# Odd attention of a two-block model: two copies change engine, and score buffers and maxima go round in longer rings

## What is computed

```python
def odd_mixer(x, w_in, w_out, ...):
    q_c, kv_c, gate_c, cq, ckv, k_rope = split_cols(x @ w_in, ODD_SPLITS)
    ...
    o_cmp, slc_score = nsa_compressed(q, kv[:, :, 0, 0], kv[:, :, 0, 1], cmp_pe, cmp_w1, cmp_w2, tbl_c)
    o_slc = nsa_selected(q, kv[:, :, 1, 0], kv[:, :, 1, 1], slc_score, tbl_c)
    o_win, _ = banded_attention(q, kv[:, :, 2, 0], kv[:, :, 2, 1], WIN_SIZE - 1, tbl_c, 1)
    o_c = gates[:, :, 0] * o_cmp + gates[:, :, 1] * o_slc + gates[:, :, 2] * o_win
    ...
    o_d = mla_attention(qd[..., :D_NOPE], rope(qd[..., D_NOPE:], pos), k_nope, rope(k_rope, pos), v)
    y = jnp.concatenate([o_c.reshape(B, S, -1), o_d.reshape(B, S, -1)], axis=-1)
    return y @ w_out
```

## Time and profile before

| | |
|---|---|
| median of three runs | 2121.37 us (2120.21 to 2123.31) |
| the profiled execution | 2128.46 us, its span 2126.7 us |
| TensorE busy | 2008.8 us, 94% of the span |
| VectorE busy | 1089.1 us, 51% |
| ScalarE busy | 959.7 us, 45% |

### The profile page before, as it was taken

One profiled execution on the slowest core, in us unless ns is written; L12 is line 12 of the kernel. 1 busy time (PEld: TensorE's weight loads), 2 busy tenths in 40 slices (PEclk: granted clock), 3 DMA queues, 4 the chain that ended last, 5 costly groups with the idle time before them and its releaser, 6 DMA issues.

```text
span 2126.7 us, 25345 instructions
## 1 busy us (share of the span) xinstructions
PE 2008.8 (94%) x9889; PEld 1494.4 (70%) x9889; DVE 1089.1 (51%) x2023; ACT 959.7 (45%) x1758; POOL 12.7 (1%) x28
## 2 busy tenths in 40 slices
PE   8999889999889999889999999999889999999997
PEld 3876446677456888566788888787655678888885
DVE  5623864632774322656655543442465576555333
ACT  4734664644674333574422222344676544322223
POOL 1000000000000000000000000000000000000000
PEclk8999889999989999999999999999999999999999
DMA  8431432223202533003233333324400123333331
GB/s 280 128 81 50 159 99 79 60 71 90 80 20 80 149 89 92 8 1 114 70 99 99 93 97 93 104 77 100 142 2 1 41 70 99 99 93 96 99 92 47
DMA packets 301268, 183.14 MB, mean 86 GB/s; under 512 B 17550, under 2 KB 292108, under 8 KB 299948
## 3 DMA queue, kind: packets, MB, share of 16 engines
q1 hardware_dynamic: 295437, 166.05, 26.7%
q10 hardware_dynamic: 4704, 13.31, 1.7%
q0 software_dynamic: 1008, 2.15, 0.3%
HBM read 179.22 MB, written 2.27 MB: 85 GB/s over the span
## 4 chain that ended last, share of the span: by engine, by line
PE 82%; DVE 8%; ACT 6%; issue 2%; DMA 1%; another core or an unknown queue 0%; ACTq 0%; DVEq 0%
PE PS L902 22%; PE PS L904 22%; PE PS L903 21%; PE PS L1048 3%; PE PS L1076 2%; PE PS L1061 2%; DVE SE L2152 1%; DVE WLO L2078 1%; PE PS L1202 1%; PE PS L1120 1%; PE PS L1225 1%; PE PS L1129 1%; PE PS L1014 1%; DVE X L2045 1%; ACT WHI L1514 1%
## 5 line engine op out<-in xcount | busy, mean ns | idle before, releaser
L903 PE MATMUL PS<-LO,WHI 128*128 128x512 f32 x1690 | 659.8, 390 | 0.0
L902 PE MATMUL PS<-HI,WHI 128*128 128x512 f32 x1578 | 626.6, 397 | 25.2 <-DVE LO L2051 10.3
L904 PE MATMUL PS<-HI,WLO 128*128 128x512 f32 x1578 | 616.7, 391 | 0.0
L2078 DVE TENSOR_TENSOR WLO<-RING,WHI 128x1024 fp32r<-128x1024 f32 (+3 forms) x271 | 314.3, 1160 | 530.9 <-ACT WHI L1514 529.9
L1514 ACT ACTIVATE WHI<-RING 128x1024 fp32r<-128x1024 f32 (+3 forms) x271 | 272.6, 1007 | 468.6 <-PE PS L904 446.7
L902 PEld LDWEIGHTS PS<-HI,WHI 128*128 128x128 f32 x1578 | 297.6, 189 | 108.5 <-issue 27.0
L903 PEld LDWEIGHTS PS<-LO,WHI 128*128 128x128 f32 x1690 | 318.5, 188 | 65.3 <-issue 1.7
L904 PEld LDWEIGHTS PS<-HI,WLO 128*128 128x128 f32 x1578 | 297.3, 188 | 62.9
L902 PE MATMUL PS<-HIDDEN,WHI 128*128 128x512 f32 x352 | 137.1, 390 | 0.6 <-PE PS L904 0.6
L904 PE MATMUL PS<-HIDDEN,WLO 128*128 128x512 f32 x352 | 137.0, 389 | 0.0
L903 PE MATMUL PS<-HIDDEN,WHI 128*128 128x512 f32 x352 | 136.9, 389 | 0.0
(11 more groups left out here) (341 smaller groups left out, 2343.1 us busy)
## 6 DMA issues: line engine op xcount, KB each, us to landing
RING<-in_ffn_w_up SPq DMA_DIRECT2D x88, 512.0 KB, 3.7
RING<-in_w_in SPq DMA_DIRECT2D x48, 512.0 KB, 3.8
RING<-in_w_mod SPq DMA_DIRECT2D x32, 512.0 KB, 4.3
RING<-in_ffn_w_down SPq DMA_DIRECT2D x32, 512.0 KB, 4.0
RING<-in_ev_w_in SPq DMA_DIRECT2D x30, 512.0 KB, 3.8
RING<-in_w_out SPq DMA_DIRECT2D x16, 512.0 KB, 4.4
RING<-in_od_w_in SPq DMA_DIRECT2D x15, 512.0 KB, 3.9
RING<-in_ffn_w_down SPq DMA_DIRECT2D x16, 384.0 KB, 3.4
```

The source lines that it names most:

```text
L902: mm(bank, WHI[i2][:, i, :], hi, start=(k == 0), stop=False)
L903: mm(bank, WHI[i2][:, i, :], lo, start=False, stop=False)
L904: return mm(bank, WLO[i2][:, i, :], hi, start=False, stop=last)
L2078: tt(WLO[i2][:, 0:nk, :], raw, WHI[i2][:, 0:nk, :], ALU.subtract).then_inc(me.signals(w_split), 1)
```

## The change

In the odd attention, VectorE takes two kinds of copies over from ScalarE: that of the small turn of each gated unit (`small_collected`), and that of the mixed values of each unit (`mixed`). The copies of a turned bank are now counted on two semaphores, `at_turn_free` for ScalarE's and `at_small_free` for VectorE's; `bank_left` says which of them a turn has to wait for. There is a third set of maxima, for both attentions. The odd attention's units go round in seven score buffers, by `SE_ODD`, where buffer 3 comes twice in eight; the three new ones lie in tiles of Z that are free in this stage, and in RS, which is made longer by 128 columns. ScalarE's `high`, which used to follow its own `mixed`, waits on `at_mixed`.

```diff
-        RS = sb("RS", [T])[:, :]
+        RS_WIDE = sb("RS", [640])
+        RS = RS_WIDE[:, 0:T]
...
-        UNIT_MAX = [TINY[:, c:c + 8] for c in (56, 152)]
+        UNIT_MAX = [TINY[:, c:c + 8] for c in (56, 152, 104)]
...
+        SE += [spare("SE4", ends["Z"] + 31 * TILE, [3 * T]), spare("SE5", ends["Z"] + 10 * TILE, [5 * T]), RS_WIDE]
+        SE_ODD = (0, 1, 2, 3, 4, 5, 6, 3)
...
+        def collected_through(at):
+            return SMALL_TURN[:at].count(False), SMALL_TURN[:at].count(True)
+
+        def bank_left(at):
+            n = max((n + 1 for n in range(at) if TURN_BANK[n] == TURN_BANK[at]), default=0)
+            if n:
+                by_act, by_dve = collected_through(n)
+                return (at_small_free, by_dve) if SMALL_TURN[n - 1] else (at_turn_free, by_act)
...
+                u["se"] = u["n"] % 4 if u["n"] < len(UNITS["even_mix"]) else SE_ODD[u["n"] % 8]
+                u["before"] = filled.get(u["se"])
+                filled[u["se"]] = u
...
                 def values(u):
-                    pe.wait_ge(at_turn_free, u["turned"])
+                    by_act, by_dve = collected_through(u["turned"])
+                    pe.wait_ge(at_turn_free, by_act)
+                    if u["gates"]:
+                        pe.wait_ge(at_small_free, by_dve)
...
                 def high(k):
-                    act.wait_ge(*me.last)
+                    if even:
+                        act.wait_ge(*me.last)
+                    else:
+                        act.wait_ge(at_mixed, len(UNITS["even_mix"]) + 4 * (k + 1))
                     inputs([H[:, k, :]], even and k < 4, k, HI_MIXED)
...
                 for i in range(n + 5):
-                    if 0 <= i - 5 < n:
+                    if even and 0 <= i - 5 < n:
                         mixed(units[i - 5])
...
-                        if x < len(turns):
+                        if x < len(turns) and not (units[i - 3]["gates"] and x == 0):
                             collect(units[i - 3], x)
...
                 def scaled(u):
-                    if u["n"] >= 4:
-                        dve.wait_ge(at_turned, every[u["n"] - 4]["turned"])
-                    buf, nmax = SE[u["n"] % 4][:, 0:2 * u["width"]].rearrange("p (a t) -> p a t", a=2), UNIT_MAX[u["n"] % 2]
-                    if u["n"] >= 2:
-                        dve.wait_ge(at_exp, every[u["n"] - 2]["exps"])
+                    if u["before"]:
+                        dve.wait_ge(at_turned, u["before"]["turned"])
+                    buf, nmax = SE[u["se"]][:, 0:2 * u["width"]].rearrange("p (a t) -> p a t", a=2), UNIT_MAX[u["n"] % 3]
+                    if u["n"] >= 3:
+                        dve.wait_ge(at_exp, every[u["n"] - 3]["exps"])
...
+                def small_collected(u):
+                    dve.wait_ge(at_turned, u["turn"] + 1)
+                    if u["ring"] >= 10:
+                        dve.wait_ge(at_values, OWNER[u["ring"] - 10]["done"])
+                    nc.vector.tensor_copy(ET_SLOTS[u["place"] % 10][0:31, 0:2, :],
+                                          PS[0:31, TURN_BANK[u["turn"]], 0:2 * B].rearrange("p (x q) -> p x q", x=2)) \
+                        .then_inc(at_small_free, 1)
+
+                def mixed(u):
+                    dve.wait_ge(at_values, u["done"])
+                    nc.vector.tensor_copy(u["dst"], PS[:, 7, 0:B]).then_inc(me.signals(at_mixed), 1)
...
-                for i in range(n + 2):
+                for i in range(n + 2 if even else n + 5):
                     if i < n:
                         scaled(units[i])
-                    if i >= 2:
+                    if not even and i >= 5:
+                        mixed(units[i - 5])
+                    if 0 <= i - 3 < n and units[i - 3]["gates"]:
+                        small_collected(units[i - 3])
+                    if 0 <= i - 2 < n:
                         normalise(units[i - 2])
```

More of the change, by code:

```diff
@@ L318, in build @@
         acc_ready, acc_free_act, acc_free_dve = sem("acc_ready"), sem("acc_free_act"), sem("acc_free_dve")
+        at_small_free = sem("at_small_free")
         at_scores, at_scaled, at_exp, at_probs, at_turned, at_turn_free, at_values, at_mixed = (
@@ L661, in build @@
         UNITS = {"even_mix": even_units(), "odd_mix": odd_units()}
-        OWNER, TURN_BANK = [], []
-        def turns_collected(at):
-            return max((n + 1 for n in range(at) if TURN_BANK[n] == TURN_BANK[at]), default=0)
+        OWNER, TURN_BANK, SMALL_TURN = [], [], []
+        def collected_through(at):
[5 more added lines that the diff above has]
+                return (at_small_free, by_dve) if SMALL_TURN[n - 1] else (at_turn_free, by_act)
         def count_units():
             n_unit = n_score = n_scaled = n_exp = n_prob = n_value = 0
-            mains, sides = [], []
+            mains, sides, filled = [], [], {}
             for u in UNITS["even_mix"] + UNITS["odd_mix"]:
                 u["n"], n_unit = n_unit, n_unit + 1
+                u["se"] = u["n"] % 4 if u["n"] < len(UNITS["even_mix"]) else SE_ODD[u["n"] % 8]
+                u["before"] = filled.get(u["se"])
+                filled[u["se"]] = u
                 for g in u["groups"]:
@@ L689, in count_units @@
                 OWNER.extend([u] * len(u["turns"]))
+                SMALL_TURN.extend(bool(u["gates"]) and i == 0 for i in range(len(u["turns"])))
                 TURN_BANK.extend(5 + (u["turn"] + i) % 2 for i in range(len(u["turns"])))
@@ L1055, in turn @@
                     at = u["turn"] + i
-                    if turns_collected(at):
-                        pe.wait_ge(at_turn_free, turns_collected(at))
-                    buf = SE[u["n"] % 4]
+                    if bank_left(at):
+                        pe.wait_ge(*bank_left(at))
+                    buf = SE[u["se"]]
                     for x, (a, c, w) in enumerate(u["turns"][i]):
@@ L1639, in exp @@
                     c += a * u["width"]
-                    x = SE[u["n"] % 4][:, c:c + w]
-                    fn(x, x, ACT.Exp, bias=UNIT_MAX[u["n"] % 2][:, at:at + 1], scale=-1.0,
+                    x = SE[u["se"]][:, c:c + w]
+                    fn(x, x, ACT.Exp, bias=UNIT_MAX[u["n"] % 3][:, at:at + 1], scale=-1.0,
                         accum_out=UNIT_DEN[u["n"] % 3][:, at:at + 1]).then_inc(at_exp, 1)
@@ L1951, in _ @@
                     elif s in ("even_out", "odd_out"):
+                        if s == "odd_out":
+                            act.wait_ge(at_mixed, sum(len(units) for units in UNITS.values()))
                         inputs(inputs_of(s)[-1:], False, len(inputs_of(s)) - 1, HI_MIXED)
@@ L2155, in normalise @@
                 def normalise(u):
-                    buf, den, rden = SE[u["n"] % 4], UNIT_DEN[u["n"] % 3], UNIT_RDEN[u["n"] % 2]
+                    buf, den, rden = SE[u["se"]], UNIT_DEN[u["n"] % 3], UNIT_RDEN[u["n"] % 2]
                     dve.wait_ge(at_exp, u["exps"])
@@ L2182, in normalise @@
                         ts(buf[:, c:c + w], buf[:, c:c + w], rden[:, at:at + 1], None, ALU.mult).then_inc(me.signals(at_probs), 1)
+                def small_collected(u):
[7 more added lines that the diff above has]
+                    dve.wait_ge(at_values, u["done"])
+                    nc.vector.tensor_copy(u["dst"], PS[:, 7, 0:B]).then_inc(at_mixed, 1)
                 def head_scaled():
```

## The result

| | before | after |
|---|---|---|
| median | 2120.45 us (five runs) | 2103.34 us (five runs, 2099.73 to 2106.03) |
| ratio, 95% interval | | 0.9909 [0.9894, 0.9923], so 16 to 22 us less |
| the profiled execution, its span | 2128.5, 2126.7 | 2106.0, 2104.2 |
| VectorE, ScalarE busy | 1089.1, 959.7 | 1102.0, 949.5 |

Faster, as forecast, but by more. The forecast was 2108.6 us, in a range of 2103 to 2117, on a base of 2121.4. By the ratio that base becomes 2102.1 us, 19.3 less, just under the range; the median by itself, 2103.34, lies at its lower end.

The account below looks back on a forecast made before the run. TensorE was nearest its bound, held up by coupling between engines. Passes 4 to 15 -12.9, hand-offs +1.2, latent 0, end +0.4, even attention -1.5: -12.8 on 2121.4 gives 2108.6 us, range 2103 to 2117.

Parts of the forecast that it names:

- What held VectorE: Odd attention's score passes: the wait on the exponentials of unit n - 2 ends last, not the turns the profile names.
- The length of a round without waits: Odd attention, four passes with no TensorE wait: 6.07 + 4.42 + 4.77 + 4.94 = 20.2 us, against an average 25.6.
- hand-offs: Odd attention: 0.1 us added back for each of 12 passes, for VectorE's new hand-offs, +1.2 us.
- Pass 4: Odd attention: this pass keeps its clock dip and its 7.8 us, since what comes before it is the same.
- Even attention: It gets the third set of maxima but not the buffers; two or three waits go, -1.5 us (0 to -2.5).
- Maxima and buffers: Odd attention: score passes start a pass sooner, needing both parts; shared buffer 3 leaves 0.4 us of stall a round.
- The copies: Moved to VectorE at 0.42 and 0.29 us: its round 16.0 to 18.2 us, ScalarE's 2.5 less.
- The start, the latent units, the end: Odd attention: small copy adds 0.35 us before pass 4, latent units 0, stage end +0.4 (0 to +2).
- A: Rival, odd attention: VectorE becomes the bound, a round is 23 us, about -8, 2113.5 us; chance 0.16.
- B: Rival, odd attention: the clock dips stay, three at 1.7 us each, -7.7, 2113.7 us; chance 0.14.
- C: Rival, latent attention, passes 19 to 35: VectorE's mixed copy gates TensorE's values, slower, 2130 us; chance 0.07.
- D: Rival, odd attention: ScalarE's exponentials, interleaved with its turn copies, set the pass; no change, 2120.5 us; chance 0.08.

Follow-up runs that it names:

- e1: The kernel before with the third set of maxima alone, in both attentions: ratio 0.9896, passes 4 to 15 in 59.93 us.
- e2: The kernel before with the seven buffers alone: ratio 0.9999, passes 4 to 15 in 75.09 us.
- e16: The changed kernel with the mixed copy on ScalarE and buffer 0 used twice instead of buffer 3: ratio 0.9882, passes 4 to 15 in 57.93 us.
- e3: The changed kernel with both copies left on ScalarE (third set of maxima and seven buffers): ratio 0.9892, passes 4 to 15 in 58.78 us.
- e14: The kernel before with the third set of maxima in the even attention alone: ratio 0.9941, passes 4 to 15 in 74.82 us.
- e17: The changed kernel itself once more, nothing altered: ratio 0.9909, passes 4 to 15 in 58.87 us.
- e8: The changed kernel with the mixed copy back on ScalarE, small copy on VectorE: ratio 0.9868, passes 4 to 15 in 58.47 us.
- e9: The changed kernel with each small copy made three times on VectorE: ratio 0.9928, passes 4 to 15 in 66.98 us.
- e10: The changed kernel with VectorE's low(6) one pass later, 34 instead of 33: ratio 0.9880, end of the stage 50.97 us.
- e4: The changed kernel with two sets of maxima again in both attentions: ratio 1.0031, passes 4 to 15 in 83.46 us.

## Why the prediction was off

**What held VectorE: right.** It was the exponentials of unit n - 2, though the profile named the turns. e1 and e2 show it from both sides. I said that the read of the exponentials' sum fills the 0.22 us before VectorE goes on; in the trace before that read ends at 1599.63, so it fills 0.09 of them and 0.13 are left.

**The length of a round without waits: the step that failed.** I put the four passes at 20.2 us. e16, where TensorE has no wait left in these passes, shows 6.06 + 3.85 + 4.77 + 4.63 = 19.3. The two passes from which I had subtracted the idle times that the timeline prints, 4.42 and 4.94, were too long; the two without a wait were right to 0.01.

The rows show what the subtraction misses. In pass 13 before, the first turn starts at 1599.08 and the score matmuls at 1600.24, 1.16 us later, of which 0.76 is printed as idle. The same pass after:

```profile
1582.17 0.41 PE L1076 MATMUL PS<-MATS,SE 128*31 128x128 f32 x2
1582.41 0.33 PE L1055 MATMUL PS<-Z 128*128 128x62 f32 x2
```

Here they start 0.24 later, before the turn's 0.41 us are over. So the wait cost 0.92 us, not 0.76: the printed idle time counts from the end of the matmul before it and leaves out the overlap that the wait takes away. The three waits of pass 13 print 1.77 us and cost 2.33.

What it did to the sum: passes 5 to 15 were forecast at 54.5 + 1.2 of stall + 1.2 of hand-offs = 56.9 us and took 52.65. Of the 4.3 us, 3 x 0.56 are the three passes of 4.42 that took 3.86. The three of 4.94 + 0.4 took 5.02, 5.03 and 4.60: 1.4. The allowance for hand-offs, for which no row spoke, is the last 1.2.

**Pass 4: wrong, 1.6 us.** I let its clock dip stay, since what comes before it is the same. It is the same (the stretch before it 13.37 in e1 and before), and the dip was gone: 6.23 in e1 and 6.22 after, against 7.81. So a dip cost 1.6, not the 1.7 that I took from pass 12. Why it went is open (last section).

**Even attention: wrong in size.** -1.5 (0 to -2.5) against -3.9, and -5.0 in e1, e3, e14 and e17 (94.79). I priced the idle times of two or three cases. There were five, 2.4 us in sum, and 1.7 of busy time went with them.

These make up the miss in the profiles: -4.3, -1.6 and -2.4 of the 9.7 us by which -22.5 exceeds -12.8 (by the ratio the miss is 6.5), with the other 1.4 in stretches that I had left out, most of them untouched code. The first stretch by itself moves by more than that from run to run.

**Maxima and buffers: half right.** I wrote that without the buffers the gain would stop at the buffer's last turn. It stops there, but over the twelve passes that costs only 1.15 us: e1 has 59.93 where e3 has 58.78. The stall that stays in seven buffers was right: 0.4 forecast; 0.39 is what pass 7 loses in e16, of which 0.2 goes with e8 and 0.2 with the buffer.

**The copies: right, but for what ScalarE gains.** 0.42 and 0.29 us forecast, 0.407 and 0.288 measured; VectorE's round 18.2 and 18.10. ScalarE's round fell by 1.9 us and not by 2.5 (18.61 to 16.75): its records overlap too (the small copy of 0.36 us at 1599.98 before is followed at 1600.25), which I had allowed for on VectorE alone. The forecast's spare in VectorE's order, 0.3 us, is what e9 gives. The Trainium skill (VectorE: DVE Perf Modes, Specifications) puts ScalarE closer to PSUM; the rows agree for both shapes, 359 against 407 ns and 274 against 288.

**The start, the latent units, the end: right.** +0.35 forecast before pass 4 and +0.32 measured; 0 and +0.4 for pass 18 on, measured as +0.4 together, and e10 shows that the end's part is low(6) ahead of the mixed copies.

**The rivals.** A, VectorE as the bound, did not happen but is near: e9's 21.1 us of work gave a round of 21.97, where A said 23 for 21.2: its 1.8 us a round for waits was about 0.9. B, dips that stay: in the kernel after none did, pass 4's went too. C: the latent units were not slowed. D, ScalarE's queue setting the pass: not with three sets. With two, e2 and e4 are that case: VectorE's wait on the exponentials stays.

## What to carry to other kernels

Where an engine waits for two things that end close together, the profile names one. Compare the end of each with the start of the waiter: the same small gap each time marks the true one (0.22, 0.23 and 0.22 us here), and only its removal paid. For a bound "without waits", take passes that have none, or compare starts with starts; passes minus the printed idle times come out too long. Work that is moved to a queue behind an instruction that waits inherits the wait: TensorE stood 0.46 us for a copy in e4, and 2.28 us at the end of the kernel after. And before a longer stage is put down to waits, its idle and busy times have to be looked at apart: e4's passes were 6.7 us longer with 0.5 us more of idle time, the rest at a lower clock.

## What the runs showed of the hardware

The clock dip is not settled by what TensorE idled just before. In e2 and in e14 the odd attention starts alike: the same pass lengths and the same idle times, 0.70 and 1.48 us, before passes 3 and 4. Both have two sets of maxima there. A microsecond from the first half of pass 4 in e2 (the pass began at 1539.68), and one in e14 (1529.78), columns as in the earlier trace rows:

```profile
1541.00:1542.00 1.00, 1.00 (x4) 0.11 (x2) 0.89 (x8) 1.00 (x3) 0.00 (x0) 0.51 0.00 0
```
```profile
1531.00:1532.00 1.00, 1.00 (x5) 0.24 (x5) 0.93 (x7) 1.00 (x3) 0.00 (x0) 1.00 0.00 0
```

Pass 4 took 7.82 in e2 and 6.23 in e14. It had the dip before, in e2, e4 and e9, and in none of the nine other experiments nor after. The kernel before and e14 even have the same program in the whole odd attention, and there the dips fell on passes 4, 5, 11 and 15 before, and on 7 and 15 in e14. The Trainium skill (TensorE: Matmul & The Clock Gate, What's actually happening) calls the slower state the default, which activity lifts. The passes fit that as a whole: 0.84 of mean clock in e4 with TensorE busy 72.75 of 83.46 us, 1.00 with 58.12 of 58.87. What decided between e2 and e14 no run here shows; it is worth 1.6 us a dip and was not tried further.
